# One-core encoder layer on Trainium2: forget block and GLA inputs of a token block loaded within the block ahead, in smaller transfers

## What is computed

```python
p = rms_norm(h, norm_pre) @ w_in     # [q | k | v | SiLU gate | gla q | gla k | gla v | gla SiLU gate | forget | gate A | gate B]
s = einsum(q, k) * HEAD_DIM**-0.5 - slope * dist;  p = exp(s - m) / (sum + exp(sink - m));  oa = p @ v
b = cumsum(la, axis=2)               # la: log of the forget gate, per token and channel
scores = einsum('bhtd,bhsd,bhtsd->bhts', q, k, decay)
o = scores @ v + (q * exp(b)) @ s0
s1 = exp(b_end) * s0 + (k * exp(b_end - b))^T @ v
y = sigmoid(ga) * ((oa * silu(za)) @ w_branch_attn) + sigmoid(gg) * ((og * silu(zg)) @ w_branch_gla)
h = h + rms_norm(y @ w_out, norm_post)
```

## Time and profile before

| | us |
|---|---|
| median of 3 runs | 2957.28 |
| lowest, highest | 2956.74, 2960.8 |
| profiled execution | 2960.62 |
| its span (first to last instruction) | 2958.8 |
| PE busy in the span | 2827.3 (96%) |
| attention stage in it, end of the projections to the first branch products | 1386 to 2152 |

### The profile page before, as it was taken

How to read it: one execution, slowest core, us unless ns; L and a number is a source line. 1 busy time by engine, 2 the same in 40 slices (tenths; PEclk the granted TensorE clock), 3 DMA queues, 4 the chain that set the end, 5 groups by cost and what they waited for, 6 DMA issues and landing times. The chain is left out here.

```text
span 2958.8 us, 51536 instructions
## 1 busy us (share of the span) xinstructions
PE 2827.3 (96%) x20490; PEld 2679.2 (91%) x20490; DVE 1992.4 (67%) x3171; ACT 1166.4 (39%) x1908; POOL 78.9 (3%) x55
## 2 busy tenths in 40 slices
PE   7999999998999999999998999999889999999996
PEld 6999999998999999999777777777789999999996
DVE  7799777777687777776667667777453332555556
ACT  5334333345354333344555555555330000343331
POOL 0122000000000000000000000000000000000001
PEclk9999999999999999999999999999999999999998
DMA  3455334345244333435455555555563333555554
GB/s 117 137 186 187 127 120 133 116 137 205 90 144 139 124 130 123 130 118 157 147 163 179 165 163 160 158 177 150 153 210 110 114 117 117 171 179 190 183 192 143
DMA packets 227187, 441.00 MB, mean 149 GB/s; under 512 B 23840, under 2 KB 134688, under 8 KB 226096
## 3 DMA queue, kind: packets, MB, share of 16 engines
q1 hardware_dynamic: 226992, 438.31, 46.0%
HBM read 358.10 MB, written 80.67 MB: 148 GB/s over the span
## 5 line engine op out<-in xcount | busy, mean ns | idle before, releaser
L1733 PE MATMUL bank<-th,w_hi 128*128 128x272 f32 x2400 | 701.0, 292 | 14.6 <-DVE w_lo L1181 7.8
L1733 PE MATMUL bank<-tl,w_hi 128*128 128x272 f32 x2400 | 695.9, 290 | 0.0
L1733 PE MATMUL bank<-th,w_lo 128*128 128x272 f32 x2400 | 695.1, 290 | 0.0
L814 ACT ACTIVATE w_hi<-w_raw 128x1024 fp32r<-128x1024 f32 x256 | 270.4, 1056 | 721.0 <-PE bank L1711 657.7
L1160 DVE TENSOR_TENSOR w_lo<-w_raw,w_hi 128x1024 fp32r<-128x1024 f32 x256 | 313.2, 1223 | 263.7 <-ACT w_hi L814 263.3
L1733 PEld LDWEIGHTS bank<-th,w_hi 128*128 128x128 f32 x2400 | 454.6, 189 | 19.7 <-DVE w_lo L1181 10.3
L1733 PEld LDWEIGHTS bank<-tl,w_hi 128*128 128x128 f32 x2400 | 454.7, 189 | 1.0 <-issue 1.0
L1733 PEld LDWEIGHTS bank<-th,w_lo 128*128 128x128 f32 x2400 | 454.1, 189 | 0.0
L837 ACT ACTIVATE w_hi<-w_more 128x1024 fp32r<-128x1024 f32 x240 | 254.6, 1061 | 474.3 <-DVE w_more L1200 253.8
L1181 DVE TENSOR_TENSOR w_lo<-w_more,w_hi 128x1024 fp32r<-128x1024 f32 x240 | 303.4, 1264 | 124.6 <-ACT w_hi L837 122.2
L1711 PE MATMUL bank<-uh,w_hi 128*128 128x272 f32 x1024 | 323.3, 316 | 18.4 <-DVE w_lo L1160 14.5
(11 more groups left out here) (205 smaller groups left out, 5078.1 us busy)
## 6 DMA issues: line engine op xcount, KB each, us to landing
w_raw<-in_w_tiles SPq DMA_DIRECT2D x376, 512.0 KB, 3.8
w_more<-in_w_tiles SPq DMA_DIRECT2D x120, 512.0 KB, 3.2
p_scratch<-stage SPq DMA_DIRECT2D x44, 544.0 KB, 2.9
gate<-gate_scratch SPq DMA_DIRECT2D x32, 544.0 KB, 4.0
gl<-p_scratch SPq DMA_DIRECT2D x8, 1536.0 KB, 9.9
qa<-p_scratch SPq DMA_DIRECT2D x8, 1152.0 KB, 8.4
gate_scratch<-stage SPq DMA_DIRECT2D x16, 544.0 KB, 3.0
gate_scratch<-stage SPq DMA_DIRECT2D x64, 136.0 KB, 3.8
```

What stands on the lines that cost most here:

```text
L814: act.activation(w_hi[:, h], w_raw[:, h], ACT.Copy).then_inc(s_whi, 1)
L1733: ins = pe.matmul(out[:, 0:GAW], wt[:, k], ut[:, k], start=start and k == 0 and i == 0, stop=stop and k == HK - 1 and i == 2, skip_group_c ...
```

## The change

The two functions become four, and their transfers are cut:

- `qa` is loaded in two parts: q and v (10 tiles, 640 KB) with `kw` at step 9 of the block ahead instead of step 12, and the gate (8 tiles, 512 KB) at step 12.
- `lac` is loaded at step 12 of the block ahead, when `lac_lo` of that block exists.
- `gl` is loaded in three parts of 8 tiles (512 KB) within the block ahead: v at step 17, q and k at step 20, the gate at step 23. Each waits for the last reader of its part.
- Step 2 keeps the store of the block before, and loads nothing.
- The readers wait for two transfers of `qa` and three of `gl` in place of one.

```diff
             def load_attention(it, nq=P):
                 ge(sp, s_sc, 8 * it)
-                ge(sp, s_zs, it)
-                settle(sp)
-                sp.dma_start(qa[:, :, 0:nq], p_dram[T_Q:T_K, :, tokens(it, nq)].rearrange("t p n -> p t n")).then_inc(s_qa, 16)
+                sp.dma_start(qa[:, 0:T_ZA, 0:nq], p_dram[T_Q:T_ZA, :, tokens(it, nq)].rearrange("t p n -> p t n")).then_inc(s_qa, 16)
...
-            def load_gla(it, nq=P):
-                ge(sp, s_og, 2 * it)
-                settle(sp)
-                sp.dma_start(gl[:, :, 0:nq], p_dram[T_GQ:N_P, :, tokens(it, nq)].rearrange("t p n -> p t n")).then_inc(s_gl, 16)
+            def load_attention_gate(it, nq=P):
+                ge(sp, s_zs, it)
+                sp.dma_start(qa[:, T_ZA:T_K, 0:nq], p_dram[T_ZA:T_K, :, tokens(it, nq)].rearrange("t p n -> p t n")).then_inc(s_qa, 16)
+
+            def load_gla(it, part, nq=P):
+                if it > 0:
+                    if part == 0:
+                        sp.wait_ge(s_gs, 4 * it)
+                    if part == 1:
+                        sp.wait_ge(s_tev, N_T * it - 3)
+                    if part == 2:
+                        sp.wait_ge(s_z2, it)
+                c = slice(8 * part, 8 * part + 8)
+                sp.dma_start(gl[:, c, 0:nq], p_dram[T_GQ + 8 * part:T_GQ + 8 * part + 8, :, tokens(it, nq)].rearrange("t p n -> p t n")).then_inc(s_gl, 16)
+
+            def load_forget(it, nq=P):
+                ge(sp, s_lcl, it)
                 sp.dma_start(lac[0:nq], la_dram[it, 0:nq]).then_inc(s_lac, 16)
...
                         if s == 2 and it > 0:
                             store_gla(it - 1)
-                            load_gla(it, nq)
...
+                        ahead = DEC if it == N_IT - 2 else P
+                        if s == 9 and it < N_IT - 1:
+                            load_attention(it + 1, ahead)
                         if s == 12 and it < N_IT - 1:
-                            load_attention(it + 1, DEC if it == N_IT - 2 else P)
+                            load_attention_gate(it + 1, ahead)
+                            load_forget(it + 1, ahead)
+                        if s in (17, 20, 23) and it < N_IT - 1:
+                            load_gla(it + 1, {17: 1, 20: 0, 23: 2}[s], ahead)
```

More of the change, by code:

```diff
@@ L602, in _ @@
             load_attention(0)
+            load_attention_gate(0)
             sp.wait_ge(s_sum, 4 * (MIX - 1) + 3)
@@ L612, in _ @@
             sp.wait_ge(s_st, 16 * MIX)
-            load_gla(0)
+            load_forget(0)
+            for part in range(3):
+                load_gla(0, part)
             recent = SEQ - WINDOW
@@ L961, in step @@
                 if s == 3:
-                    act.wait_ge(s_qa, 16 * it + 16)
+                    act.wait_ge(s_qa, 32 * it + 32)
                     ge(act, s_z2, it)
@@ L1001, in step @@
                 if s == 19:
-                    act.wait_ge(s_gl, 16 * it + 16)
+                    act.wait_ge(s_gl, 48 * it + 48)
                     act.wait_ge(s_zs, it + 1)
@@ L1464, in step @@
                     if hh == 0:
-                        dve.wait_ge(s_gl, 16 * it + 16)
+                        dve.wait_ge(s_gl, 48 * it + 48)
                     e = ex[:, hh % 2, 0:nch]
@@ L1823, in step @@
                 if s == 0:
-                    pe.wait_ge(s_qa, 16 * it + 16)
+                    pe.wait_ge(s_qa, 32 * it + 32)
                     ge(pe, s_tev, N_T * it)
@@ L1893, in step @@
                     half = (s - 11) // 2
-                    pe.wait_ge(s_gl, 16 * it + 16)
+                    pe.wait_ge(s_gl, 48 * it + 48)
                     pe.wait_ge(s_tev, N_T * it + (9, 11)[half])
```

## The result

The changed kernel takes **2940.69 us** (median of 4 runs, 2939.59 to 2941.15) against 2959.04 us (4 runs, 2956.74 to 2961.85) for the kernel before: a ratio of **0.9937**, 95% interval 0.992 to 0.9954, so 18 us faster. Forecast were 2940.7 us. The span of the profiled execution fell from 2958.8 to 2938.5 us.

A forecast was written before the change was run, and what follows sets the result against it. PE was taken as the bound, busy 2827.3 of 2958.8 us. Waits 6.0, block 8 3.5, clock 6.9 and 1.7, less costs 1.5, gave 16.6 us off 2957.3: 2940.7 us, range 2931 to 2954.

The forecast's parts named there:

- Rival 1: Step 9: PE's wait stays because another producer is late next; only block 8's 3.5 us gained, 2955 us; chance 0.14.
- rival 4: Slot 8's weight: moved loads queue up again behind one another, so it stays as late; 2958 us; chance 0.05.
- Rival 2: Behind step 9: waits shrink, but each remaining 1.35 us still costs a low-clock stretch; 2947.5 us; chance 0.24.
- The constant of 1.35 us: PE's wait for `lac_lo` at step 9: the part ACT and DVE need in any case, beside the weight's lateness.
- The lateness counted in the earlier trace: ACT's waits for slot 8's weight in blocks 1 and 3 to 7, set to zero: 6.0 us gained.
- The clock: PE at 1.2 GHz behind step 9's waits, outside block 8: 24.0 us falls to 10.2, gaining 6.9 us (1.8 to 12.0).
- Costs that I put too low: Late weight in block 2 and remake pieces in block 6, less a gain in block 4: 1.5 us, bounds -1.2 and +3.6.
- The start: Stage's start, block 0: the same bytes go out in another order; 0, and 0.5 us either way.
- The gain that I gave the attention part in block 4: Block 4: remake pieces wait 1.19 us behind the issue of `kw`, which moves away; set against the costs.
- Block 8: Weight found in time by ACT: all 3.5 us of PE's wait gained, plus 1.7 us of clock.
- Rival 3: Slots 22 and 24: parts of `gl` delay weight loads, ACT 4.7 us late in blocks 1 to 8; 2978 us; chance 0.07.
- every issue behind a part takes under 1 us: SP's queue in the profile after: each issue following a part of `gl` is short, under 1 us.

The follow-up runs named there:

- the repetition: The changed kernel itself, run again in the second group of runs and compared with the kernel before: 2940.57 us, ratio 0.9942.

## Why the prediction was right, and where its terms were off

**The mechanism** holds in each part that was tested. The lateness of one weight sets PE's wait: removing the bytes ahead of it gives the gain, other bytes in their place take it away, half of them don't outside block 8, and a delay on ACT without any transfer brings back waits and low stretches. Rival 1 (the wait stays) and rival 4 (nothing moves) fell with the profile after: the waits read 1.22 to 1.24 us. Rival 2 (the clock stays low) fell too.

**The constant of 1.35 us** was 0.12 too high: without a late weight the wait is 1.23. The difference is what the lateness adds beyond ACT's own wait. The lateness counted in the earlier trace rows was 6.0 us; PE's waits in blocks 1 and 3 to 7 fell from 2.62, 2.55, 2.24, 1.62, 2.42 and 2.61 to 1.22 to 1.24, by 6.7 us. The sum is good to a tenth, but not each block: the prediction read the constant off blocks 3, 5 and 7 alone, and block 6 has it too. In block 1 the difference of the two waits is 1.00 us, since PE's wait stops growing (last section), and in block 4 it is 1.65, since a second weight is late there (ACT waits 0.20 us at 1749.76). These two errors, 0.35 us down and 0.30 us up, nearly cancel, which is luck.

**The clock** was the term that I mis-sized. I let each remaining wait of 1.35 us keep half a stretch, 10.2 us at 1.2 GHz in all, and gained 6.9 us. None was left: 24.0 us at the lower level before, 0 after, so 12.0 us, the upper end that I gave. The 14 profiles of this study have 84 such waits outside blocks 0 and 2. Behind the 59 of up to 1.58 us the clock never fell; behind or within 18 of the 25 from 1.62 to 2.63 us it fell, for 3.4 or 6.8 us. A wait of 1.3 us is therefore on the safe side, where I had set it in the middle. That a stretch costs half its length was right: 1.6 us for 3.4.

**Costs that I put too low** took this back. Six blocks gained 17.6 us (6.7 and 12.0 would be 18.7; blocks 3 and 6, whose stretch of 6.8 us begins 0.6 and 0.4 us before the wait ends, show 4.1 and 3.9 where 4.7 and 4.6 are expected), against 12.9 less 1.5. Block 2 lost 2.4 us: its weight was late by 2.55 us instead of 0.62, as the third of `gl` and four pieces stand ahead of it; I had foreseen the place, and 1 us of it. The start, put at 0 within 0.5, lost 1.3 us with the time ahead of block 0 in this profile; in that of the repetition block 1 starts at 1471.15, before at 1471.34, so this is scatter. The gain that I gave the attention part in block 4 didn't exist. Block 8 gained 6.3 against 5.2; ACT still waits 0.85 us there for its weight at 2062.92, where I expected none. The sum forecast was 16.6 and the spans differ by 20.4, the medians by 18.4. That the forecast time meets the measured one to 0.1 us is luck: the median of before rose from 2957.28 to 2959.04 with one more run, and the gain, 1.8 us larger than forecast, came out of errors that partly cancel (clock 5.1 us and block 8 1.1 us better, block 2 2.4 us lost).

**Rival 3** (the parts hold up the weights of the block's end) has a real mechanism, as the run with `gl` whole shows, but its price was wrong: 38 us forecast, 7 us measured. One part is the hold, 5.1 us in the rival's sum and 1.8 to 3.3 us for the weight behind a whole `gl` (5.3 for a remake piece issued at once behind it), so that ACT waited 1.8 to 2.5 us in blocks 1 and 3 to 6 and not 4.7. The other is that each us of ACT's lateness was to cost PE a us. Between ACT's split and PE's use lie about 2 us of cover at that place: ACT waits 2.48 us and PE 0.53, and in block 2 of that kernel 6.13 and 4.19. The blocks whose weight was late by 1.8 to 2.5 us are still 0.7 to 0.9 us longer, block 6 by 1.7, so something smaller than this wait is lost too; which waits, I didn't follow. It would not have made the kernel slower than before even with the whole transfer there.

**The size of a transfer.** The prediction's statement that every issue behind a part takes under 1 us was nearly right: one took 1.21 us, the weight of block 2, behind a part and four pieces, and at the stage's start, which the prediction left out, a store behind `lac` and all three parts took 3.08 us. Its 1.8 us for a part were a third of the 5.4 us of the whole, so its rows could not show that parts move at the rate of the whole, nor that the queue hides a fixed cost; the run with the parts at step 2 does. The rule of the Trainium skill that I set against the change (page "DMA: Bandwidth & Descriptors", sections "Anatomy of one DMA — SWDGE (gpsimd) path" and "Rules for kernel authors": 1 MiB or more in one DMA, about 2.0 us of fixed cost) is a rule for the greatest bandwidth, and the cost stands there for DMAs that GpSimd issues; all of this kernel's are issued by SP. By an estimate from the page's figure, two further fixed costs paid in the queue would make the weight behind `gl` in three parts at step 2 some 4 us later in each block. ACT was 0.3 us later in the mean, and the ratio is 1.0001. So most of such a cost, if it is there, is hidden between transfers in the queue. A whole `gl` at step 23 is slower than its parts at steps 17, 20 and 23 by 7 us, by place and size together.

## What to carry to other kernels

When an engine with an ordered list waits for something small, follow the chain back until a queue: here the name in the list of waits was the forget block, and the cause a weight behind 1792 KB of other loads. Bytes ahead of an urgent load are free up to its slack and costly from there on, so spread them over places with slack, and price a late load at the engine that is the bound, not at the one that waits first. Where waits of the matrix engine are between 1.6 and 2.6 us, look at the clock behind them: in this kernel the clock fell behind most of them and behind none of 1.58 us or less, and a stretch of 3.4 us at 1.2 GHz cost 1.6 us on top of the wait.

## What the runs showed of the hardware that I had not expected

- The clock's fall depends on the wait's length more sharply than I took it to: none of 59 waits of 1.22 to 1.58 us, 18 of 25 of 1.62 to 2.63 us. It isn't certain even at one length: of six waits of 2.07 or 2.08 us in one execution five were followed by a low stretch and one wasn't.
- SP's issue is held by what is queued ahead, not by the size of one transfer: in block 3 the next weight took 3.94 us to issue behind 1792 KB, 2.00 behind 1536 KB (the forget block alone moved) and 0.34 behind 896 KB (up to 0.96 in block 1); three parts of 512 KB in a row took 0.86, 1.76 and 2.03 us. How long the issue takes also depends on when it is asked for. Counted from the start of the large issue, SP was free again after 6.1 us where `lac` followed 1536 KB at once (5.14 us for its issue), after 5.8 where the weight followed 2.9 us later, and after 7.8 behind 1792 KB; with `gl` whole at step 23 it was 4.5 to 5.9 us.
- When ACT is later than some 1.3 us, PE's wait at step 9 doesn't grow further: it reads 2.61 to 2.63 us for a lateness of 1.25 to 1.67 us in ten waits of three kernels. The time is lost all the same, ahead of that wait. In the kernel with three parts at step 2, without a low stretch in either block, the lateness is 1.29 us in block 1 and 1.62 in block 3; the transposes of `pb` ahead of step 9 begin 27.87 and 28.17 us after the block's start, step 9 itself 31.11 and 31.44, and the blocks are 78.73 and 79.06 us long.
